# Routed experts of a hybrid decoder step: token rows held in the array while weights stream, 16 weight slots, and sample-token products spread over the array

## The chip, the cores and the metric

The kernel runs on one core of a Trainium2 chip. The metric is the time of one execution on the device in microseconds (us); lower is better. All arithmetic is float32.

## The reference, cut to what matters

Two layers run for a prompt of 256 positions and for 8 sample tokens that carry states and caches: 264 token rows of 1024 values. Layer 0 has a mixer of state-space (SSD) and retention heads, layer 1 a mixer of pooling and convolution. Both then have cross attention to a memory of 256 rows; layer 0 ends in a dense SwiGLU, layer 1 in eight routed experts.

```python
def cross_attn(h, mk, mv, wq, wo):            # sample tokens: mk, mv from a cache per token
    q = (h @ wq).reshape(bsz, seq, X_HEADS, X_HEAD_DIM)
    p = softmax(einsum('blhd,bmhd->bhlm', q, mk) * X_HEAD_DIM ** -0.5)
    return einsum('bhlm,bmhd->blhd', p, mv).reshape(bsz, seq, 1024) @ wo

def moe(h, rw, rb, w1, w3, w2):               # w1, w3: 8 x 1024 x 1792, w2: 8 x 1792 x 1024
    top_v, top_i = lax.top_k(t @ rw + rb, 2)
    gates = softmax(top_v)
    for e in range(8):
        out += combine[:, e:e+1] * ((silu(t @ w1[e]) * (t @ w3[e])) @ w2[e])
```

In layer 0 every sample token b also updates its SSD state (128 x 1024) and its retention state and reads one row of output from each.

## The kernel before, in words

The five engines run programs written by hand, tied by semaphores. PE runs the matrix products; ACT and DVE take results out of PSUM; SP issues nearly all weight loads, POOL those of states, caches and outputs. A float32 product appears in the trace as two matmul records and two weight loads, so counts there are twice those in the code.

**PSUM.** Banks 0 to 5 rotate over named groups in the order of `psum_groups` (`begin`, `end`, `taken`, `full`). Banks 6 and 7 (`SUMS`) hold sums over the sample tokens.

**Weights of the trunk.** `weight_items` lists blocks of 256 columns (1 MB each); SP streams them through six slots of the ring (`TRUNK_RING`), each load waiting until the slot's last block has been used. Slots 6 to 10 hold states and, in cross attention, cache rows (`kv`, five buffers; POOL issues each load at L721 when a buffer is free).

**Sample tokens.** `sample_x` (L968) spreads a token's row over 128 partitions by a product with a column of the identity, in two halves; POOL has decayed the token's state (L676), DVE adds the update, and `sample_y` (L950) multiplies the state by the token's vector, 8 columns wide. `sample_v` and `sample_o` (L1070, L1057) do the same for retention. In `cross`, for every token the query row is spread the same way (L1189) and DVE multiplies it into the cached keys (L2015). In layer 0 the eight parts of the product `xv0` (L1147) are placed between the tokens. After the softmax the probabilities multiply the cached values (L1230): 16 records of 8 x 256 per token. `clear_sums` (L1047) zeroes the sums first, ACT copies them out (`sums_out`, L1473), and the output projection `xo` (L831) follows.

**Experts.** The router's rows are scattered by expert into `expert_rows` in DRAM, 96 rows (`CAP`) for each expert. PE, ACT and DVE loop over four pairs of experts, SP over single experts. For expert n, PE holds a 128 x 64 piece of the weights and streams the 96 token columns of `hg` (L1369), with two such pieces side by side in the array; gate and up come out with hidden units on partitions. ACT takes SiLU (L1606), DVE multiplies (L2210) into `ehid`. PE then turns the next expert's rows (`turn_rows`, L1333), and the down step holds `ehid` and streams the weights: 64 tokens at a time, two column strips side by side (L1387), then the other 32 tokens, four strips side by side (L1393), first for four chunks and then for the other four (`DOWN`). ACT and DVE copy the result out, ACT stores it.

**Chunks.** An expert's weights are 22 chunks (`CHUNKS`): 12 of four k-tiles by 512 columns for gate and up, two of eight k-tiles by 256 columns, eight for down. They pass through 11 slots. SP waits for a slot's release (`expert_left`) and issues the load that reuses it (`expert_load`, L556); the first 11 chunks are loaded while layer 1's attention ends.

Of the kernel before, what the change touches and what calls it, by code (L numbers as in the profile page):

```python
# [29 lines left out]
BLOCKS = ((0, 4), (4, 4), (8, 4), (12, 2))  # L30
DOWN = ((0, 2), (2, 2), (4, 2), (6, 1), (7, 2), (9, 2), (11, 2), (13, 1))
CHUNKS = 22
# [127 lines left out]
def psum_groups():  # L160
# [54 lines left out]
    def cross(l):  # L215
        r = lin_ss(f"xq{l}", KT, CROSS_NORM[l])
        r += [("qs", l, 0), ("qs", l, 1)]
        r += [("S", l, lt, hp) for lt in range(2) for hp in range(2)]
        for b in range(NB):
            r += [("qb", l, b, j) for j in range(2)]  # L220
            if l == 0:
                r += [("xv0", b // 2, b % 2)]
# [20 lines left out]
def trunk_kernel(nc, w, consts, outs):  # L243
# [8 lines left out]
    with ctx:  # L252
# [23 lines left out]
        slot_full = [sem(f"slot_full{s}") for s in range(RING)]  # L276
# [4 lines left out]
        base_full = [16 * sum(i % TRUNK_RING == s for i in range(len(items))) if s < TRUNK_RING else 0 for s in range(RING)]  # L281
# [106 lines left out]
        R.at = max(xr_at, (FT + 2) * T)  # L388
        memtok = R.take(2, DM)
# [38 lines left out]
        R = Region()  # L428
        ehid = R.take(ET, CAP)
        esil = R.take(2, 4, CAP)  # L430
        hg = R.take(2, KT, CAP)
        htok = R.take(3, DM)
        xtok = R.take(3, DM)
        xe = R.take(DM)
        ys = R.take(2, DM)
        back = R.take(2, 3, DM)
        fgain = R.take(DM)
        fin, fsq = view(0, 3, DM), htok[:, 0, :]
# [13 lines left out]
        fss = R.take(3, 1)  # L452
        idx = sb("idx", [P, 3, NE], U32)
# [6 lines left out]
        zeros = small[:, 64:64 + 2 * NB]  # L460
# [44 lines left out]


        @block.sync
        def _(sp):
# [36 lines left out]
            def expert_load(e, j):  # L545

                pick = slice(e, e + 1) if isinstance(e, int) else bass.ds(e, 1)
                if j < 12:
                    b, kh = j // 4, j % 2
                    src, k, n = ups[j % 4 // 2][:, pick, 4 * kh:4 * kh + 4, b * 512:(b + 1) * 512], 4, 512  # L550
                elif j < 14:
                    src, k, n = ups[j - 12][:, pick, :, 1536:1792], 8, 256
                else:
                    f0, k = DOWN[j - 14]
                    src, n = down[:, pick, f0:f0 + k, :], DM
                sp.dma_start(slot_view(j, k, n), src.rearrange("p e t n -> p (e t) n")).then_inc(slot_full[j % RING], 16)  # L556

            def expert_left(n, j):

                if j < 12 and j % 2 == 0:  # L560
                    sp.wait_ge(chunk_done, n * 13 + (j // 2 + 1))
                elif j < 14:
                    sp.wait_ge(sem("up_full" if j in (3, 7, 11, 13) else "gate_full"), n * 4 + (min(j // 4, 3) + 1))
                elif j < CHUNKS - 1:
                    sp.wait_ge(chunk_done, n * 13 + (j - 14 + 7))
                else:
                    sp.wait_ge(sem("down_full"), n + 1)
# [5 lines left out]

            sp.wait_ge(sem("aos_done"), 2)
            for j in range(TRUNK_RING, RING):
                expert_load(0, j)
            for j in range(TRUNK_RING):
                slot_left(sp, last_in_slot[j])
                expert_load(0, j)
# [3 lines left out]
            steps = sp.value_load(rounds[0:1, 1:2], min_val=NE - 1, max_val=3 * NE - 1)  # L583
            with sp.Fori(0, steps) as n:
                e, e_next = n & (NE - 1), (n + 1) & (NE - 1)

                sp.wait_ge(slot_full[0], e + e_next + 1)
                sp.wait_ge(sem("rows_turned"), n + 1)
                rows_load(n + 1)
                for j in range(RING, CHUNKS):  # L590
                    if j != 14:
                        expert_left(n, j - RING + (j == 13))
                    expert_load(e, j)
                for j in range(RING):
                    expert_left(n, j + RING)
                    expert_load(e_next, j)
            sp.wait_ge(sem("rows_turned"), sp.snap(steps + 1))
            rows_load(0)
            for j in range(RING, CHUNKS):
                expert_left(steps, j - RING)  # L600
                expert_load(NE - 1, j)
# [9 lines left out]
        def _(pool):  # L611
# [10 lines left out]
            nc.gpsimd.memset(zeros, 0.0).then_inc(sem("zeros_set"), 1)  # L622
# [129 lines left out]
            load(pw[:, :, :], w["pool_w"][0].rearrange("g c d -> c g d"), "pw_in")  # L752
# [21 lines left out]
            load(fgain, w["norm_final"].unsqueeze(0).to_broadcast([P, DM]), "fgain_in")  # L774
# [9 lines left out]
            for c in range(3):  # L784
                n = P if c < 2 else NB
                for j in range(2):
                    pool.indirect_dma_start(back[0:n, j, c, :], None, xg[:, :], bass.IndirectOffsetOnAxis(ap=rowi[0:n, c, j:j + 1], axis=0))\
# [5 lines left out]
        def _(pe):  # L793
# [101 lines left out]
            pe.wait_ge(sem("dt_ready"), 1)  # L895
# [48 lines left out]
            def sample_y(b):  # L944
# [4 lines left out]
                for g in range(SG):  # L949
                    ins = mm(psum[0:NB, SUMS + g, :], Zc[:, g, b * NB:(b + 1) * NB], hb[:, b % 3, g * 512:(g + 1) * 512],  # L950
                             start=(b == 0), stop=(b == NB - 1), skip_group_check=True)
# [9 lines left out]
            def sample_x(b):  # L961

                if b == 0:
                    taken(pe, ("xstok", 0))
                    taken(pe, ("xstok", 1))
                for g in range(SG):
                    o = begin(("xb", b, g))
                    end(("xb", b, g), mm(o, ident[0:NB, b:b + 1].to_broadcast([NB, P]), xstok[0:NB, g * 512:(g + 1) * 512],  # L968
                                         start=True, stop=True))
# [75 lines left out]
            def clear_sums(n, bank_no):  # L1045

                mm(psum[0:n, SUMS + bank_no, :], zeros[:, 0:n], cbase[:, 0:512], start=True, stop=False, skip_group_check=True)  # L1047

            def sample_o(b):

                taken(pe, ("vb", b))
                if b == 0:
                    pe.wait_ge(sem("q_spread"), 1)
                    pe.wait_ge(sem("zeros_set"), 1)
                    clear_sums(2 * NB, 0)
                for hh in range(RH // 2):
                    ins = mm(psum[0:2 * NB, SUMS, hh * RV:(hh + 1) * RV], Zq[:, hh, b * 2 * NB:(b + 1) * 2 * NB],  # L1057
                             rb[:, b % 4, hh * RV:(hh + 1) * RV], start=False, stop=(b == NB - 1), skip_group_check=True)
# [106 lines left out]
            def cross(l):  # L1165
# [18 lines left out]
                taken(pe, ("qs", l, 0))  # L1184
                taken(pe, ("qs", l, 1))
                for b in range(NB):
                    for j in range(2):
                        o = begin(("qb", l, b, j))
                        end(("qb", l, b, j), mm(o, ident[0:NB, b:b + 1].to_broadcast([NB, P]), qstok[0:NB, j * 512:(j + 1) * 512],  # L1189
                                                start=True, stop=True))  # L1190
                    if l == 0:
                        tokmajor("xv0", [b])
# [30 lines left out]
                clear_sums(NB, 0)  # L1223
                clear_sums(NB, 1)
                taken(pe, ("pT", l))
                for b in range(NB):
                    rows = kv_in(pe, l, NB + b)
                    for h in range(XH):
                        for m in range(2):
                            ins = mm(psum[0:NB, SUMS + h // 2, (h % 2) * 256:(h % 2 + 1) * 256], Zp[:, m * XH + h, b * NB:(b + 1) * NB],  # L1230
                                     rows[:, m, h * 256:(h + 1) * 256], start=False, stop=(b == NB - 1 and m == 1),
# [1044 lines left out]
```

## Time and profile before

| | |
|---|---|
| three timed runs | 1691.6 us median (1689.88 to 1698.04) |
| the profiled execution | 1685.52 us, its span 1683.7 us |
| PE busy | 1540.6 us, 92% of the span |
| HBM read | 339 MB |
| mean granted TensorE clock | 0.947 of full speed |

The profile shows one execution. A chain of waits follows the work that ended last backwards from the end; each piece in it is time that nothing else covered. "Issue" is waiting for which the profile has no event on that engine, such as a DMA's arrival or the fetch of instructions. A window gives the busy time of each engine in a stretch, the granted clock, the DMA engines' busy share (modelled, it can exceed 1) and GB/s.

### The profile page before, as it was taken

The numbers are of one execution on the slowest core, as the hardware profiler recorded it, in microseconds if no ns is written. First come the engines' busy times: TensorE is split into PE (matmuls) and PEld (weight loads), VectorE is DVE, ScalarE is ACT, GpSimd is POOL, SyncE is SP. The second block draws the span as 40 slices with busy tenths as digits, with TensorE's granted clock in tenths as the row PEclk, the third lists the DMA queues.
The fourth block names the chain that finished last, engine by engine and source line by source line (L and its number), as shares of the span: only waits on it lengthen the run. The fifth ranks groups of instructions, "written<-read, shape, count | busy, mean of one in ns | idle before, by whom it ended". The sixth has DMA issues, their size and how long they took to land.

```text
span 1683.7 us, 30260 instructions
## 1 busy us (share of the span) xinstructions
PE 1540.6 (92%) x13352; PEld 1199.3 (71%) x13352; DVE 469.0 (28%) x1264; ACT 183.3 (11%) x382; POOL 125.5 (7%) x156
## 2 busy tenths in 40 slices
PE   7999989899999999999998999959988998998983
PEld 5886557588765888878877764749658667776771
DVE  3436473530340211141278353230000000000002
ACT  2121012101110100000012210020000000000001
POOL 3003412400010200000000001010000000000001
PEclk9997989799999999999999988969999999999997
DMA  9643543554472795435434336638999999999882
GB/s 279 195 152 88 150 113 107 163 188 169 137 269 100 269 393 181 140 107 167 150 128 150 103 110 237 225 124 303 320 362 360 330 351 359 336 344 369 326 320 87
DMA packets 217321, 368.81 MB, mean 219 GB/s; under 512 B 8883, under 2 KB 134091, under 8 KB 217040
## 3 DMA queue, kind: packets, MB, share of 16 engines
q1 hardware_dynamic: 195112, 292.47, 50.5%
q0 software_dynamic: 19264, 71.22, 12.3%
q10 hardware_dynamic: 2816, 3.15, 0.6%
q8 instruction: 112, 1.84, 0.4%
q14 instruction: 17, 0.14, 0.0%
HBM read 339.12 MB, written 28.49 MB: 218 GB/s over the span
## 4 chain that ended last, share of the span: by engine, by line
PE 88%; DVE 5%; issue 4%; POOL 1%; DMA 1%; ACT 1%; ACTq 0%; POOLq 0%; SPq 0%; DVEq 0%
PE psum L831 29%; PE psum L1369 19%; PE psum L1253 9%; PE psum L1147 7%; PE psum L1387 6%; PE psum L1230 3%; PE psum L1393 3%; DVE ring L2015 1%; PE psum L950 1%; PE psum L968 1%; PE psum L1189 1%; PE psum L1215 1%; PE psum L1181 1%; PE psum L986 1%; PE psum L940 1%
## 5 line engine op out<-in xcount | busy, mean ns | idle before, releaser
L1369 PE MATMUL psum<-arena,ring 128*64 128x96 f32 x7168 | 318.6, 252 | 47.1 <-issue 46.2
L1369 PEld LDWEIGHTS psum<-arena,ring 128*64 128x64 f32 x7168 | 310.7, 141 | 56.9 <-issue 56.8
L831 PE MATMUL psum<-hT,ring 128*128 128x264 f32 x1168 | 270.3, 394 | 2.8 <-issue 1.6
L831 PEld LDWEIGHTS psum<-hT,ring 128*128 128x128 f32 x1168 | 224.6, 193 | 48.3 <-issue 7.5
L831 PE MATMUL psum<-arena,ring 128*128 128x264 f32 x992 | 227.0, 392 | 9.3 <-ACT arena L1569 5.0
L831 PEld LDWEIGHTS psum<-arena,ring 128*128 128x128 f32 x992 | 191.3, 193 | 43.8 <-ACT arena L1569 5.8
L1253 PE MATMUL psum<-hT,ring 128*128 128x264 f32 x704 | 157.0, 386 | 0.0
L1253 PEld LDWEIGHTS psum<-hT,ring 128*128 128x128 f32 x704 | 133.8, 190 | 22.9
L1147 PE MATMUL psum<-ring,arena 128*128 128x256 f32 x512 | 113.7, 382 | 0.0
L2210 DVE TENSOR_TENSOR arena<-arena,psum 128x384 f32<-128x384 f32 (+1 forms) x32 | 16.1, 504 | 348.7 <-PE psum L1369 348.7
L1147 PEld LDWEIGHTS psum<-ring,arena 128*128 128x128 f32 x512 | 97.0, 191 | 19.0 <-issue 6.1
L1679 DVE TENSOR_TENSOR arena<-psum,rstd 128x264 f32<-128x264 f32 (+3 forms) x117 | 44.0, 394 | 233.6 <-PE psum L1253 118.8
L1387 PE MATMUL psum<-ring,arena 128*64 128x512 f32 x448 | 99.7, 596 | 0.0
L1387 PEld LDWEIGHTS psum<-ring,arena 128*64 128x64 f32 x448 | 30.7, 137 | 59.0 <-issue 58.1
L1230 PE MATMUL psum<-ring,arena 128*8 128x256 f32 x256 | 55.6, 379 | 0.0
L1685 DVE TENSOR_TENSOR xT<-xT,psum 128x264 f32<-128x264 f32 x40 | 17.2, 429 | 136.1 <-PE psum L831 136.0
L1393 PE MATMUL psum<-ring,arena 128*32 128x256 f32 x896 | 51.7, 381 | 0.0
L2015 DVE CUSTOM_DVE_ANT_0 ring<-ring,psum 128x256 f32<-128x256 f32 x128 | 44.6, 417 | 16.8 <-PE psum L1189 16.8
L1393 PEld LDWEIGHTS psum<-ring,arena 128*32 128x32 f32 x896 | 27.5, 110 | 29.5 <-issue 13.0
L1606 ACT ACTIVATE arena<-psum 128x384 f32<-128x384 f32 (+1 forms) x32 | 14.4, 450 | 305.3 <-PE psum L1369 305.3
L2122 DVE SCALAR_TENSOR_TENSOR arena<-arena,par 128x256 f32<-128x256 f32 x120 | 47.6, 479 | 0.0
L1230 PEld LDWEIGHTS psum<-ring,arena 128*8 128x8 f32 x256 | 23.0, 90 | 33.1 <-issue 1.4
(390 smaller groups left out, 1047.7 us busy)
## 6 DMA issues: line engine op xcount, KB each, us to landing
ring<-in_moe_w_dram SPq DMA_DIRECT2D x160, 1024.0 KB, 9.2
ring<-in_ffn_w_dram SPq DMA_DIRECT2D x30, 1024.0 KB, 5.4
ring<-in_w_in_even_dram SPq DMA_DIRECT2D x22, 1024.0 KB, 5.3
ring<-in_cache_mem_k_dram POOLq DMA_DIRECT2D x16, 1024.0 KB, 8.3
ring<-in_cache_mem_v_dram POOLq DMA_DIRECT2D x16, 1024.0 KB, 5.5
expert_rows<-arena POOLq DMA_DIRECT2D x1, 9216.0 KB, 47.9
ring<-in_w_out_even_dram SPq DMA_DIRECT2D x8, 1024.0 KB, 5.0
ring<-in_xattn_k_dram SPq DMA_DIRECT2D x8, 1024.0 KB, 4.9
```

The costliest lines, as they stand in the source:

```text
L831: ins = mm(outs_[m][0:mw, 0:T], wv[:, k, m * mw:(m + 1) * mw], rhs(base + k), start=(base + k == 0), stop=(kc == len(chunks) - 1 and k == ...
L940: ins = mm(o[:, q * P:(q + 1) * P], ident[0:SH, h:h + 1].to_broadcast([SH, P]), acT[0:SH, c * P:(c + 1) * P], start=True, stop=True)
L1147: ins = mm(o[:, 0:256], mT[:, k, m * P:(m + 1) * P], wv[:, k, :], start=(k == 0), stop=(k == KT - 1))
L1230: ins = mm(psum[0:NB, SUMS + h // 2, (h % 2) * 256:(h % 2 + 1) * 256], Zp[:, m * XH + h, b * NB:(b + 1) * NB], rows[:, m, h * 256:(h + 1) ...
L1253: ins = mm(o[:, 0:T], wv[:, k, m * P:(m + 1) * P], hT[:, k, :], start=(k == 0), stop=(k == KT - 1))
L1369: ins = mm(o[c0:c0 + 64, m * CAP:(m + 1) * CAP], wv[:, k, m * P + c0:m * P + c0 + 64], hg[:, h, kh * kn + k, :], start=(kh == 0 and m == 0 ...
L1387: mm(psum[64 * d:64 * d + 64, 4, :], ehid[:, f0 + f, 0:64], wv[:, f, d * 512:(d + 1) * 512], start=(f0 + f == 0), stop=(f0 + f == ET - 1))
L1393: ins = mm(psum[32 * d:32 * d + 32, 5, 0:256], ehid[:, f0 + f, 64:CAP], wv[:, f, d * 256:(d + 1) * 256], start=(f0 + f == 0), stop=(f0 + f ...
L1679: return v.tensor_tensor(dst, src, rstd[0:src.shape[0], a:b], ALU.mult)
L1685: free((name, t), v.tensor_tensor(xT[:, t, :], xT[:, t, :], bank((name, t))[:, 0:T], ALU.add), wait=True)
L2015: ins = v.tensor_tensor_reduce(kh, kh, bank(key)[:, q * 256:(q + 1) * 256], 1.0, 0.0, ALU.mult, ALU.add, sS[:, m, b * XH + h:b * XH + h + 1])
L2122: v.scalar_tensor_tensor(out=mixo[:, OT + t, 0:NP], in0=gp[:, t, k:k + NP], scalar=gain("ccw", 4 * k + t), in1=mixo[:, OT + t, 0:NP], op0= ...
```

## The change

Gate and up now hold the token rows and stream the weights, as the down step did: first 64 tokens with two strips side by side, then 32 tokens with four. The result has tokens on partitions, so after SiLU and the product PE transposes it (`turn_block`) into the form that the down step needs. Gate and up go in two blocks of 1024 and 768 columns; their chunks are two k-tiles of 1024 or 768 columns, so an expert has 24 chunks. The slots become 16: five more lie in the arena, where earlier buffers are dead; five chunks are loaded before the last attention ends. SP loops over pairs too. Every chunk of gate and up is read twice and released after its second reading.

The sample products are regrouped: where a product has 8 or 16 output rows, its four column quarters go to four strips of 32 output partitions; spread rows are copied by ACT to partitions 32, 64 and 96, and each spreading product takes another strip of input rows. `clear_sums` goes. In layer 0 the parts of `xv0` come after every second token. The gain row of the last norm is loaded under the semaphore on which the router's product waits. Semaphores are merged.

```diff
-BLOCKS = ((0, 4), (4, 4), (8, 4), (12, 2))
-CHUNKS = 22
+BLOCKS = ((0, 1024), (1024, 768))
+DOWN = ((0, 2), (2, 2), (4, 2), (6, 2), (8, 2), (10, 2), (12, 1), (13, 1))
+CHUNKS = 24
+MOE_RING = 16
...
+        slot_at = (mem_at, mem_at + SLOT, tail_at, tail_at + SLOT, 0)
...
+        def picked_row(r, b):
+            return const("ident")[32 * r:32 * r + NB, 32 * r + b:32 * r + b + 1].to_broadcast([NB, P])
...
+                if j < 16:
+                    (f0, n), q = BLOCKS[j // 8], j % 4
+                    src, k = ups[j % 8 // 4][:, pick, 2 * q:2 * q + 2, f0:f0 + n], 2
...
+            full(sp, ("xv1", 3, 1))
+            for j in range(2):
+                expert_load(0, j, j)
+            full(sp, ("wout1", KT - 1))
+            sp.wait_ge(sem("odd_out"), 64)
+            for j in range(2, 4):
+                expert_load(0, j, j)
+            full(sp, ("S", 1, 1, 1))
+            expert_load(0, 4, 4)
             sp.wait_ge(sem("aos_done"), 2)
...
-            load(fgain, w["norm_final"].unsqueeze(0).to_broadcast([P, DM]), "fgain_in")
+            load(fgain, w["norm_final"].unsqueeze(0).to_broadcast([P, DM]), "router_in")
...
-                for g in range(SG):
-                    ins = mm(psum[0:NB, SUMS + g, :], Zc[:, g, b * NB:(b + 1) * NB], hb[:, b % 3, g * 512:(g + 1) * 512],
+                for j in range(4):
+                    ins = mm(psum[32 * j:32 * j + NB, SUMS, 0:256], Zc[:, j // 2, b * NB:(b + 1) * NB],
...
+                    r = 2 * (b % 2) + g
+                    end(("xb", b, g), mm(o, picked_row(r, b), xstok[32 * r:32 * r + NB, g * 512:(g + 1) * 512], start=True, stop=True))
...
-                    if l == 0:
-                        tokmajor("xv0", [b])
+                    if l == 0 and b % 2:
+                        tokmajor("xv0", [b - 1, b])
...
-                clear_sums(NB, 0)
-                clear_sums(NB, 1)
...
-                    for h in range(XH):
-                        for m in range(2):
-                            ins = mm(psum[0:NB, SUMS + h // 2, (h % 2) * 256:(h % 2 + 1) * 256], Zp[:, m * XH + h, b * NB:(b + 1) * NB],
+                    for m in range(2):
+                        for h in range(XH):
+                            ins = mm(psum[32 * h:32 * h + NB, SUMS, 0:256], Zp[:, m * XH + h, b * NB:(b + 1) * NB],
...
-            pe.wait_ge(sem("router_in"), 32)
+            pe.wait_ge(sem("router_in"), 48)
...
+                    def up_block(g, b):
+                        f0, fn = BLOCKS[b]
+                        j0 = 8 * b + 4 * g
+                        wide, narrow = fn // 2, fn // 4
+                        for q in range(4):
+                            arrive(j0 + q)
+                            wv = weights(j0 + q, 2, fn)
+                            for k in range(2):
+                                for c in range(2):
+                                    mm(psum[64 * c:64 * c + 64, 3 * b + g, 0:wide], hg[:, h, 2 * q + k, 0:64],
+                                       wv[:, k, c * wide:(c + 1) * wide], start=(q == 0 and k == 0), stop=(q == 3 and k == 1))
+                        for q in range(4):
+                            wv = weights(j0 + q, 2, fn)
+                            for k in range(2):
+                                for c in range(4):
+                                    ins = mm(psum[32 * c:32 * c + 32, 3 * b + 2, g * 256:g * 256 + narrow], hg[:, h, 2 * q + k, 64:CAP],
+                                             wv[:, k, c * narrow:(c + 1) * narrow], start=(q == 0 and k == 0),
+                                             stop=(q == 3 and k == 1), skip_group_check=True)
+                            if q < 3:
+                                ins.then_inc(chunk_done, 1)
...
+                    up_block(0, 0)
+                    up_block(1, 0)
+                    up_block(0, 1)
+                    turn_block(0)
+                    up_block(1, 1)
+                    pe.wait_ge(sem("ys_low"), n + 1)
+                    pe.wait_ge(sem("ys_high"), n + 1)
+                    down_part(0)
+                    turn_block(1)
                     pe.wait_ge(sem("rows_in"), n * 16 + 32)
                     turn_rows()
+                    down_part(1)
...
-                src = psum[0:n, SUMS:SUMS + banks, :].rearrange("p a b -> p (a b)")
-                af(dst[0:n, :], src, ACT.Copy).then_inc(sem("sums_out"), 1)
+                for j in range(4):
+                    ins = af(dst[0:n, j * width:(j + 1) * width], psum[32 * j:32 * j + n, SUMS, 0:width], ACT.Copy)
+                ins.then_inc(sem("sums_out"), 1)
...
+                taken(act, ("qs", l, 0))
+                taken(act, ("qs", l, 1))
+                for r in range(1, 4):
+                    af(qstok[32 * r:32 * r + NB, :], qstok[0:NB, :], ACT.Copy).then_inc(sem("q_copied"), 1)
```

`turn_block` transposes four or three 128 x 128 pieces of the 64-token rows and two or four of the 32-token rows; ACT then copies the first into `ehid`, DVE the second.

## Rows read from the trace of the kernel before

**Rows 1.** The page: busy time, and the chain's share by line.

```profile
PE 1540.6 (92%) x13352; PEld 1199.3 (71%) x13352; DVE 469.0 (28%) x1264; ACT 183.3 (11%) x382; POOL 125.5 (7%) x156
...
PE psum L831 29%; PE psum L1369 19%; PE psum L1253 9%; PE psum L1147 7%; PE psum L1387 6%; PE psum L1230 3%; PE psum L1393 3%; DVE ring L2015 1%; PE psum L950 1%; PE psum L968 1%; PE psum L1189 1%; PE psum L1215 1%; PE psum L1181 1%; PE psum L986 1%; PE psum L940 1%
```

**Rows 2.** Groups by line and shape: busy us, mean ns of one | idle before.

```profile
L1369 PE MATMUL psum<-arena,ring 128*64 128x96 f32 x7168 | 318.6, 252 | 47.1 <-issue 46.2 <-DVE arena L2198 0.9
...
L1387 PE MATMUL psum<-ring,arena 128*64 128x512 f32 x448 | 99.7, 596 | 0.0
...
L1393 PE MATMUL psum<-ring,arena 128*32 128x256 f32 x896 | 51.7, 381 | 0.0
...
L2015 DVE CUSTOM_DVE_ANT_0 ring<-ring,psum 128x256 f32<-128x256 f32 x128 | 44.6, 417 | 16.8 <-PE psum L1189 16.8
...
L1057 PE MATMUL psum<-ring 128*16 128x128 f32 x64 | 11.7, 346 | 5.7 <-DVE ring L1901 5.6
```

**Rows 3.** Windows of the expert stage: engines' busy us, clock, DMA share, GB/s.

```profile
1136.60:1656.70 520.10, 473.89 (x8576) 374.51 (x8576) 23.58 (x47) 27.19 (x51) 0.00 (x0) 0.97 0.92 330
...
1224.00:1236.00 12.00, 10.46 (x248) 10.11 (x246) 0.56 (x1) 0.49 (x1) 0.00 (x0) 1.00 1.03 408
...
1211.00:1215.00 4.00, 2.58 (x63) 2.39 (x57) 0.00 (x0) 0.49 (x1) 0.00 (x0) 1.00 1.03 247
1249.00:1251.00 2.00, 2.00 (x44) 1.23 (x40) 0.00 (x0) 0.00 (x0) 0.00 (x0) 1.00 0.06 7
```

**Rows 4.** Chain in the expert stage: start us, us, what.

```profile
1223.01 5.50 PE psum L1369 x127
...
1241.86 0.81 PE psum L1333 x8
1242.67 6.16 PE psum L1387 x28
1248.83 3.16 PE psum L1393 x56
...
1261.30 5.46 issue
```

**Rows 5.** Chain through the values product of layer 1.

```profile
1033.28 1.81 PE psum L1047 x4
1035.10 27.64 PE psum L1230 x128
...
1062.76 1.02 ACT arena L1473
```

**Rows 6.** Timeline: the first cache load that waits for that product.

```profile
1038.86 0.70 POOL L721 DMA_DIRECT2D ring<-in_cache_mem_v_dram  x1 [14.16 <-PE psum L1230]
```

**Rows 7.** The tile ring, 980 to 1066 us: its loads' landing.

```profile
DMA to landing us min/median/max: 5.2/5.4/13.7
```

**Rows 8.** Chain in layer 0's attention: scores, then the query spread and xv0.

```profile
440.78 6.91 PE psum L1181 x32
447.69 1.91 PE psum L1189 x4
449.60 3.65 PE psum L1147 x16
```

**Rows 9.** Chain in the SSD stage: spread rows and state products.

```profile
163.91 3.14 PE psum L950 x4
...
199.06 1.91 PE psum L968 x4
200.97 1.81 PE psum L950 x4
```

**Rows 10.** Timeline: the gain row's load.

```profile
1097.78 0.58 POOL L613 DMA_DIRECT2D arena<-in_norm_final_dram  x1
```

**Rows 11.** Line 613 from 1090 to 1130 us: landing of its three loads.

```profile
DMA to landing us min/median/max: 6.1/6.4/7.5
```

**Rows 12.** Chain: the router's product.

```profile
1103.46 3.56 PE psum L1301 x16
```

More of the change, by code:

```diff
@@ L280, in trunk_kernel @@
         xg_slots = xg.rearrange("(n s) d -> s n d", s=CAP)
-        base_full = [16 * sum(i % TRUNK_RING == s for i in range(len(items))) if s < TRUNK_RING else 0 for s in range(RING)]
+        base_full = [16, 48, 16 * 13] + [0] * (MOE_RING - TRUNK_RING - 3)
+        base_full += [16 * sum(i % TRUNK_RING == s for i in range(len(items))) for s in range(TRUNK_RING)]
         class Region:
@@ new lines, in turn_block @@
+                    def turn_block(b):
+                        pe.wait_ge(sem("hid_tok"), n * 2 + (b + 1))
+                        for t in range(BLOCKS[b][1] // 256):
+                            tr(psum[:, 3 * b, t * P:(t + 1) * P], tok64[b][:, t * P:(t + 1) * P], ident)
+                        if b == 0:
+                            for t in range(2):
+                                ins = tr(psum[:, 1, t * P:(t + 1) * P], tok32[0][:, t * P:(t + 1) * P], ident)
+                        else:
+                            at = TOK32_B
+                            tr(psum[:, 4, 0:P], arena[:, at:at + P], ident)
+                            tr(psum[:, 4, P:2 * P], arena[:, at + 64:at + 192], ident)
+                            tr(psum[0:64, 4, 2 * P:3 * P], arena[:, at + 128:at + 192], ident)
+                            ins = tr(psum[:, 4, 3 * P:4 * P], arena[:, at - 64:at + 64], ident)
+                        ins.then_inc(sem("hid_turned"), 1)
@@ new lines, in down_part @@
+                    def down_part(part):
+                        j0 = 16 + 4 * part
+                        pe.wait_ge(sem("ehid_64"), n * 2 + (part + 1))
+                        pe.wait_ge(sem("ehid_32"), n * 2 + (part + 1))
+                        for q, (f0, fn) in enumerate(DOWN[4 * part:4 * part + 4]):
+                            arrive(j0 + q)
+                            wv = weights(j0 + q, fn, DM)
+                            for f in range(fn):
+                                for d in range(2):
+                                    mm(psum[64 * d:64 * d + 64, 6, :], ehid[:, f0 + f, 0:64], wv[:, f, d * 512:(d + 1) * 512],
+                                       start=(f0 + f == 0), stop=(f0 + f == ET - 1))
+                        for q, (f0, fn) in enumerate(DOWN[4 * part:4 * part + 4]):
+                            wv = weights(j0 + q, fn, DM)
+                            for f in range(fn):
+                                for d in range(4):
+                                    ins = mm(psum[32 * d:32 * d + 32, 7, 0:256], ehid[:, f0 + f, 64:CAP], wv[:, f, d * 256:(d + 1) * 256],
+                                             start=(f0 + f == 0), stop=(f0 + f == ET - 1))
+                            ins.then_inc(sem("down_full") if part and q == 3 else chunk_done, 1)
```

287 lines of the change are left out of this document (135 added, 152 removed).

## The prediction

> **What bounds the kernel now.** I read the page first: PE is busy for 92% of the span, and the chain that ends last lies on PE's lines almost throughout [rows 1]. So PE time that nothing else covers is worth its full price; what matters is where PE works and where it only waits. Then the groups by line: they show that almost all of PE's idle time in the expert stage stands in front of L1369, 46.2 of 47.1 us as "issue", that is, waits for a DMA or for instructions [rows 2]. Third, the windows of that stage: it takes 520.1 us, at 330 GB/s on average [rows 3]. In a stretch in which, by SP's order, down chunks pass (rows of 4 KB), the DMA engines move 408 GB/s; in one in which the two chunks of 256 columns (rows of 1 KB) pass, 247 GB/s at about the same busy share; and at 1249 us, early in a down part, they move 7 GB/s while PE works: all 11 slots are held, and none is released before the part's second reading [rows 3]. Last the chain, for the length of each piece at full clock [rows 4, 5, 8, 9].
>
> So the expert stage is bound by PE and DMA in turn. PE's own work for an expert: 896 records of L1369 at 5.50/127 = 43.3 ns, 38.8 us; down 2 x (6.16 + 3.16) = 18.6; `turn_rows` 0.8 [rows 4]. Together 58.2, times eight 466. The other 54 us of the 520 are 47 idle and some 8 at the half clock, 1.2 GHz (mean granted clock 0.97 [rows 3]; L1369 is busy for 318.6 us [rows 2], at 43.3 ns it would be 310.4). Of the 47, three stops of some 5.4 us stand where PE's loop goes back [rows 4], 16.3 in all; 30 are waits for weights.
>
> **Part 1, gate and up the other way round.** The new product is that of the down step, so its price is that of L1387 and L1393. Block 0, gate: 8 k-tiles x 2 strips x 2 records = 32 of 512 columns at 6.16/28 = 0.220, 7.04 us; 64 of 256 columns at 3.16/56 = 0.0564, 3.61 us [rows 4]. Gate and up: 21.3. Block 1 has three quarters of the columns: 16.0 if the time goes with the columns, 21.3 if not at all. A pair of records of L1369 takes 86.7 ns for 96 columns, 0.90 ns a column; one of L1387 440 ns for 512, 0.86. So it goes with the columns nearly down to 96: I take 16.1. Thirteen transposes at 0.81/8 = 0.10, a little more for 128 columns than for 96: 1.5. Down 18.6 and `turn_rows` 0.8 stay. Sum 58.3 against 58.2: **the product itself gives nothing**; it was already packed.
>
> New waits. `turn_block(0)` waits for SiLU and product of block 0, while PE has the whole gate of block 1 (8 us) before it; `turn_block(1)` has the first down part (10.7) before it. Behind `turn_block(1)` only `turn_rows` (0.8 us) covers one ACT copy and four short DVE copies. Queued behind this wait is the second down part, and behind that the next expert. I take 1.0 us an expert for this and for starting transposes; the bounds are 0 and 3 (every copy exposed at about 0.5).
>
> On changes of shape the rows say this: in a down part PE goes from two strips to four and back, and still pays 0.86 to 0.88 ns a column, less than L1369, which does not change shape [rows 4]. The Trainium skill, TensorEngine Tiling (Array Packing), Key Properties, says that changing the tiling mode drains the engine, and the new order has some 16 such changes in an expert where there were about six. It gives no price there; by the rows it is too small to see, and the sum keeps none.
>
> **Part 2, chunks and slots.** An expert is 22.02 MB; at 408 GB/s [rows 3] 54.0 us, below PE's 59.3. The rows of 1 KB go; 768 columns make rows of 3 KB, which the trace does not have. Bounds: 408 and 247 GB/s for these 6.29 MB, so 54.0 to 64.0 us; I take the upper rate, since the stretch with 408 has rows of 4 KB and only rows of 1 KB were slow. Sixteen slots hold 14.7 MB when the stage begins, so 161.5 MB are left: 396 us at 408 GB/s, and 466 with the slow price for 3 KB. PE needs 475. The phase at work holds four slots; twelve may run ahead of it, against seven before, so a dead time as at 1249 us should not come back. The 30 us of waits go.
>
> The loop still goes back three times: 16.3 stay. The half clock's 8.2 I also keep. SP now goes back three times instead of seven; its queue holds over ten chunks, some 30 us of DMA, so a stop of SP is covered. Early loads (five chunks behind the trunk's last weights, in SP's order) go out while layer 1's scores are made; they cost nothing unless they delay cache rows, by 2.6 us for one of 1 MB.
>
> Stage: 8 x 59.3 + 16.3 + 8.2 = 499 against 520: **-21** (-30 to +5).
>
> **Part 3, values product (L1230), both layers.** Now 1.81 + 27.64 us lie on the chain alone [rows 5]. In four strips a token's 16 records cost 16 x 0.0564 = 0.90, as four strips do in L1393, 7.2 for eight. But there are five buffers: the loads for tokens 5, 6 and 7 go out only when tokens 0, 1 and 2 are done. What is late next is that DMA: the first issue came 0.3 us after token 0 was done (1035.10 + 27.64/8 = 1038.56, issued at 1038.86 [rows 5, 6]); then 5.4 to landing [rows 7]. So 0.9 + 0.3 + 5.4 = 6.6, two more at 2.6 each (1.05 MB at 408), 11.8, last token 12.7. Four ACT copies instead of one of 1.02 [rows 5]: +0.5 (0 to 3). PE idles between the last tokens, so I charge 2 us of half clock for the start of the projection. 29.4 - 12.7 - 0.5 - 2 = 14.2 a layer: **-28** (-18 with a landing of 13.7 [rows 7] in both layers, -32 at best).
>
> **Part 4, spread of the query in layer 0.** PE alternates 1.91 and 3.65 [rows 8]. Four products now use four strips of input rows. No row shows that such strips overlap; column strips do. Bounds for two tokens: 3.82 as now, 0.96 if all four overlap; times four, 0 to -11.5. With overlap in twos it is -7.6; I take **-9**, since column strips come close to full overlap. DVE's 8 x 0.35 us a token [rows 2], 5.6 for two, stays below PE's 8.3. In layer 1 DVE is the bound: nothing. The three ACT copies (3.1 us at 1.02 [rows 5]) hide behind the scores, 6.91 [rows 8]; without that cover they would cost 3.1 a layer. The Trainium skill, TensorE: Matmul & The Clock Gate, Part 3, reports a speedup of 3.07 for four row tiles of 512 columns; by that the estimate is 3.82 - 1.24, times four, -10.3. No run here shows it yet.
>
> **Part 5, SSD and retention.** `sample_y` 1.81 becomes 8 x 0.0564 = 0.45, `sample_x` 1.91 becomes 0.96 if two overlap [rows 9]. In two steps the product takes 3.14 because PE waits for DVE there; what lies before that wait gives nothing, nor does token 0. Six of eight y and five of eight x count: 8.2 + 4.8, less 1.4 for token 7, whose product must wait for DVE's update: **-11** (-5 to -13). Retention: L1057 is busy for 11.7 us, three quarters could go, but half of its tokens wait for DVE and POOL: **-3.5** (0 to -8).
>
> **Part 6, the gain row.** The router's product now waits for it: issued at 1097.78, landing at most 7.5 later [rows 10, 11], 1105.3, against a start at 1103.46 [rows 12]: **+1.8** (0 to +2). The rest (merged semaphores, the fill that goes) is off PE's path.
>
> **Sum.** -21 - 28 - 9 - 11 - 3.5 + 1.8 = -70.7. The profiled execution took 1685.5 us, 1.8 more than its span; after: 1615. The runs' median lies 6.1 higher, 1691.6; on it the forecast is **1621 us**.
>
> **Rivals.**
> *Strips of input rows do not overlap.* For: nothing in the trace shows that they do. Parts 4 and 5 lose 9 + 4.8: 1635.
> *The expert stage gains nothing*, since the short cover behind `turn_block(1)`, or 3 KB rows at 247 GB/s, take the 30 us again. For: 466 us of DMA would leave little room beside PE's 475. Against: four slots of 16 held, 408 GB/s. 1621 + 21 = 1642.
> *Slower: the new rows load badly.* The place is the stage's DMA. The other parts save 50, so it decides from 570 us for 161.5 MB, 284 GB/s. At 247 for all rows: 654 us, 134 more than now: 1691.6 + 134 - 50 = 1776. Against: 408 GB/s with rows of 4 KB.
> *The loop's going back is cheaper too*, since PE's loop is shorter and the DMA engines less full: up to -16, 1605.
>
> **How the numbers follow.** Chances: forecast 0.60, strips 0.15, stage without gain 0.15, slower 0.03, cheaper loop 0.07. The range from 1602 to 1648 takes in all of these but the slow one; some tail is left out on either side, where two of them fall together or a part reaches its bound. Half a per cent, 8 us, is about what a measurement of this kernel can tell from no change. Faster 0.95, same 0.02, slower 0.03.
>
> **What would show it.** In the new profile: the stage at about 499 us with idle time before gate and up only where the loop goes back; no window near 7 or 247 GB/s; the values product at 12 to 14 us with gaps before tokens 5 to 7; four spread products in about 1 to 1.9 us; the router's product about 2 us later after the norm. Wrong it would be if the new gate and up pay more than 0.9 ns a column, if PE still waits for chunks, or if products on other strips of input rows follow one another.

## The result, and the profile after

The changed kernel takes 1621.7 us (median of four runs, 1619.0 to 1627.2); the kernel before, beside it, 1692.2 (1689.9 to 1698.0). The ratio is 0.9589, with a 95% interval from 0.957 to 0.961. The forecast was 1621, but the hit is partly luck: several of its steps were wrong or mis-sized, and their errors nearly cancel.

The profiled executions tell a little less than the medians: 1685.5 before and 1627.2 after, 58.3 us apart, where the medians are 70.5 apart. The profiled execution after was the slowest of its four. A second profile of the same kernel (the run "again" below) has a span of 1613.9 instead of 1625.4, and like the profile before it lies some 6 us below its median.

The page after (busy time; the chain's share by engine; PE's instruction packets: number, MB, share):

```profile
PE 1481.6 (91%) x9382; PEld 1020.6 (63%) x9382; DVE 477.1 (29%) x1304; ACT 201.2 (12%) x419; POOL 125.5 (8%) x155
...
q8 instruction: 80, 1.31, 0.3%
...
PE 86%; DVE 6%; issue 2%; DMA 2%; POOL 1%; ACT 1%; ACTq 0%; POOLq 0%; SPq 0%; DVEq 0%
```

The chain is still PE's [rows 1], with 9,382 instructions of PE instead of 13,352. Matching events of the traces give where the 58.3 us came from, beside the terms of the sum; the last column is the second profile:

| part | forecast | measured | second profile |
|---|---|---|---|
| expert stage, 520.1 to 491.5 (488.3) | -21 | -28.6 | -31.8 |
| values product, two layers (-11.7, -10.1; then -11.6, -14.9) | -28 | -21.8 | -26.5 |
| query spread, layer 0 | -9 | -11.2 | -11.2 |
| SSD and retention | -14.5 | +1.7 | +0.2 |
| gain row | +1.8 | +0.3 | +0.1 |
| elsewhere | 0 | +1.3 | -0.8 |
| sum | -70.7 | -58.3 | -69.8 |

So one kernel's parts differ by up to 5 us from one execution to the next, and a smaller difference in one part tells nothing.

**Expert stage.** The window of the stage after, with the columns of [rows 3]:

```profile
1106.17:1597.68 491.51, 475.94 (x4584) 213.68 (x4584) 31.17 (x87) 34.26 (x67) 0.00 (x0) 0.98 0.90 342
```

PE is busy for 475.9 us, 2 more than before [rows 3]: the product itself gives nothing, as forecast. What went is idle time. The waits of the stage after, in total, times, longest:

```profile
PE psum L1390 <- issue: 14.0, 3, 5.1
```

The three are where PE's loop goes back; the chain shows one, and the half clock behind it (10.09 us for 32 records that take 7.02 elsewhere):

```profile
1225.48 5.05 issue
1230.53 10.09 PE psum L1390 x32
```

**Values product**, chain of layer 0: the first token, the wait for the last token's load, the last token, the transposes of the sums, then the projection. [rows 5] has the same place in layer 1 before.

```profile
493.95 1.09 PE psum L1252 x16
...
497.18 8.41 DMA ring<-in_cache_mem_v_dram
...
505.64 1.94 PE psum L1252 x16
...
509.28 1.01 PE psum L990 x8
...
510.59 31.61 PE psum L863 x128
```

**Query spread**, chain of layer 0, the four products of two tokens; the xv0 products between take 7.10 for two. [rows 8] has 1.91 for the two of one token:

```profile
466.34 1.07 PE psum L1214 x8
```

**SSD.** The second of its four steps, before and after, as the chain has it: spread rows (L968, L1000), state products (L950, L982), decay rows (L940, L972), y products (L986, L1017), the state's product (L997, L1028), the z projection. Before:

```profile
156.50 1.91 PE psum L968 x4
158.41 1.81 PE psum L950 x4
160.22 1.98 PE psum L940 x16
...
167.06 2.24 PE psum L986 x16
169.30 0.91 PE psum L997 x2
170.21 7.12 PE psum L831 x32
177.33 1.91 PE psum L968 x4
```

After:

```profile
156.92 1.06 PE psum L1000 x4
157.98 0.55 PE psum L982 x8
158.53 1.10 PE psum L972 x8
...
164.23 3.65 PE psum L1017 x16
167.87 1.81 PE psum L1028 x2
169.68 8.16 PE psum L863 x32
177.85 1.06 PE psum L1000 x4
```

The regrouped products are as short as forecast, and the y products start 7.3 us after the step's beginning instead of 10.6. But the step takes 20.9 us, as before (20.8): from the y products on everything is longer. The windows of that step after, from the decay rows on (granted clock third from the end), say why:

```profile
159.63:164.23 4.60, 2.64 (x21) 1.06 (x20) 4.55 (x13) 1.47 (x3) 3.80 (x3) 0.70 1.07 314
164.23:169.68 5.45, 5.45 (x19) 4.42 (x20) 3.07 (x5) 0.00 (x0) 2.87 (x3) 0.50 0.33 80
169.68:177.85 8.17, 8.17 (x35) 6.50 (x33) 0.69 (x1) 0.39 (x1) 1.39 (x1) 0.88 0.38 114
```

In the first window VectorE is busy for 4.55 of 4.60 us and PE for 2.64: PE waits for the decay products. Then the clock is at 0.50, 1.2 GHz, while PE works without a gap.

### The profile page after: what moved, and what is told of

Same layout as the page of the kernel before. It is cut to its first block, busy times and chain, and to the rows that moved or that the text cites. A ratio compares the mean times of both kernels' runs of the same rounds, so it can differ in the third digit from the quotient of the medians.

```text
span 1625.4 us, 22293 instructions
## 1 busy us (share of the span) xinstructions
PE 1481.6 (91%) x9382; PEld 1020.6 (63%) x9382; DVE 477.1 (29%) x1304; ACT 201.2 (12%) x419; POOL 125.5 (8%) x155
## 4 chain that ended last, share of the span: by engine, by line
PE 86%; DVE 6%; issue 2%; DMA 2%; POOL 1%; ACT 1%; ACTq 0%; POOLq 0%; SPq 0%; DVEq 0%
PE psum L863 31%; PE psum L1390 13%; PE psum L1275 10%; PE psum L1172 7%; PE psum L1396 6%; PE psum L1429 6%; PE psum L1435 3%; DVE ring L2083 1%; DMA ring<-in_cache_mem_v_dram 1%; PE psum L1239 1%; PE psum L1206 1%; PE psum L1017 1%; DVE ring L1873 1%; PE psum L1407 1%; PE psum L1323 0%
## 5 line engine op out<-in xcount | busy, mean ns | idle before, releaser
L1390 PE MATMUL psum<-ring,arena 128*64 128x384 f32 (+1 forms) x704 | 137.2, 541 | 0.0
L1390 PEld LDWEIGHTS psum<-ring,arena 128*64 128x64 f32 x704 | 49.1, 137 | 80.0 <-issue 80.0
L1390 PE MATMUL psum<-arena 128*64 128x512 f32 (+1 forms) x320 | 72.1, 602 | 14.8 <-issue 14.0
L2277 DVE TENSOR_TENSOR arena<-arena,psum 128x512 f32<-128x512 f32 (+1 forms) x16 | 9.9, 621 | 252.1 <-PE psum L1396 252.1
L1396 PE MATMUL psum<-ring,arena 128*32 128x256 f32 (+1 forms) x1408 | 71.4, 354 | 0.0
L1429 PE MATMUL psum<-ring,arena 128*64 128x512 f32 x288 | 64.4, 594 | 0.8 <-issue 0.8
L1396 PEld LDWEIGHTS psum<-ring,arena 128*32 128x32 f32 x1408 | 44.1, 110 | 30.2 <-issue 11.3
L1390 PEld LDWEIGHTS psum<-arena 128*64 128x64 f32 x320 | 23.7, 149 | 56.5 <-issue 56.5
L1429 PEld LDWEIGHTS psum<-ring,arena 128*64 128x64 f32 x288 | 22.2, 137 | 37.1 <-issue 35.7
L819 POOL DMA_INDIRECT arena<-expert_rows,rowi x6 | 5.6, 934 | 505.9 <-ACTq L1691 504.4
```

Of the source, the lines that this page charges most:

```text
L1390: mm(psum[64 * c:64 * c + 64, 3 * b + g, 0:wide], hg[:, h, 2 * q + k, 0:64], wv[:, k, c * wide:(c + 1) * wide], start=(q == 0 and k == 0), ...
L1396: ins = mm(psum[32 * c:32 * c + 32, 3 * b + 2, g * 256:g * 256 + narrow], hg[:, h, 2 * q + k, 64:CAP], wv[:, k, c * narrow:(c + 1) * narro ...
L1429: mm(psum[64 * d:64 * d + 64, 6, :], ehid[:, f0 + f, 0:64], wv[:, f, d * 512:(d + 1) * 512], start=(f0 + f == 0), stop=(f0 + f == ET - 1))
```

## The experiments

Each is compared with the kernel before in runs beside it; 1689.6 to 1690.9 us is its median there. Edits are shortened. The order follows the questions.

**The SSD stage: theory A, the half clock takes the gain; rival B, something else costs it.** Three kernels, the first the changed one once more.

> The changed kernel once more, unaltered, as the measure for the three kernels that run beside it on the same chip. Both theories expect 1617 to 1625 us, the SSD stage ending (start of the first g projection) at about 227 us of the span.

Measured: 1622.0 us, ratio 0.9601 (0.9581 to 0.9622).

> The sample products of the SSD stage alone are put back as they were before (both spread rows and both state products on one strip, one wide copy of the sums, no copies of the sample rows); all else as changed. Theory A, that PE now waits for VectorE in this stage and pays the time saved back at the half clock: within 3 us of the changed kernel, SSD stage ending at 225 to 228 us, spread rows 1.9 and state products 1.8 us again, y products 1.9 to 2.3 and z products 7.1 again. Rival B, that the regrouping saves its 11 us and something else that was changed beside it costs as much: 11 us slower than the changed kernel, stage ending at 238.

```diff
-for j in range(4):
-    mm(psum[32*j:32*j+NB, SUMS, 0:256], Zc[:, j//2, ...], hb[:, b%3, j*256:(j+1)*256], ...)
+for g in range(SG):
+    mm(psum[0:NB, SUMS+g, :], Zc[:, g, ...], hb[:, b%3, g*512:(g+1)*512], ...)
-pe.wait_ge(sem("x_copied"), 3)
-mm(o, picked_row(r, b), xstok[32*r:32*r+NB, ...], ...)
+mm(o, picked_row(0, b), xstok[0:NB, ...], ...)
```

Measured: 1621.2 us, ratio 0.9594 (0.9572 to 0.9616): no difference from the changed kernel, where B asked for 11 us. B falls by the time. In its profiled execution the stage ends later than A had it, at 231 us (226.9 and 225.5 in the two profiles of the changed kernel), with y products of 3.61 in the second step: the clock can drop there with the old products too.

> The changed kernel, and on PE ahead of each wait for VectorE's decay products 9, 9, 4 and 3 idle products of 128 x 256 into an unused bank (some 0.4 us each at full clock), whose results nothing reads. Theory A (the half clock after the wait takes the gain): y products 3.65 to about 2.0, z products of the first two steps 8.2 to 7.1, stage ending 7 to 10 us earlier than in the changed kernel, at 217 to 220 us; what of that reaches the end is 5 to 10 us, unless the retention stage waits for GpSimd's stores anyway (then less). Rival B (it is not the clock): the fillers only add work, 0 to 3 us slower.

```diff
+fill((9, 9, 4, 3)[s])   # mm(psum[:, SUMS+1, 0:256], ident, cbase[:, 0:256], start=True, stop=True)
 for j in range(2):
     pe.wait_ge(sem("s_ready"), 2 * s + j + 1)
```

Measured: 1614.9 us, ratio 0.9562 (0.9542 to 0.9582), 7.2 us faster than the changed kernel. The windows of the same step:

```profile
161.29:165.38 4.09, 4.09 (x21) 3.63 (x21) 4.05 (x7) 0.83 (x2) 1.54 (x1) 1.00 0.75 218
165.38:168.02 2.64, 2.64 (x19) 2.16 (x19) 1.30 (x2) 0.00 (x0) 0.49 (x1) 1.00 0.02 8
168.02:175.14 7.12, 7.12 (x34) 5.80 (x33) 0.69 (x1) 0.39 (x1) 3.77 (x3) 1.00 0.52 147
```

PE even starts the y products 1.8 us later (9.1 us behind the step's beginning), but at full clock they and the state's product take 2.64 us instead of 5.45, the projection 7.12 instead of 8.17, the step 18.8 instead of 20.9. The stage ends at 220.5 us. A holds: useless work in a wait buys the time that the regrouping had earned.

> As the kernel with fillers in the SSD stage, and 4, 3, 3 fillers ahead of the cache waits of tokens 5, 6 and 7 of the values product in both layers and 4 ahead of the transposes of its sums. Theory A: the output projection after it takes 28.8 us instead of 31.6 and 31.3, the last token's products and the transposes go at full clock: 3 to 4 us a layer, 6 to 8 us faster than with the SSD fillers alone. Rival: the loads end the product and the projection is slow for another reason, such as its weights: no difference.

```diff
+fill((0, 0, 0, 0, 0, 4, 3, 3)[b])
 rows = kv_in(pe, l, NB + b)
 ...
+fill(4)
 o = begin(("aoT", l))
```

Measured: 1611.1 us, ratio 0.9541 (0.952 to 0.9562), the fastest version; 3.8 us faster than the SSD fillers alone, against 6 to 8 expected. The projection runs at full clock in both layers; layer 0:

```profile
504.94 28.75 PE psum L863 x128
```

What lies ahead of it is not shorter in layer 0: from the end of the prompt's attention product to the projection 17.8 us instead of 17.3, although the last token takes 1.05 us instead of 1.94. So the loads set it.

**The values product.**

> The values product of both layers alone is put back: its 128 products on one strip with 8 output rows each into two banks, one wide copy of the sums. Theory, from the changed kernel's trace (V product gave 11.7 and 10.1 us): 20 to 24 us slower than the changed kernel, product 27.6 us on the chain, output projection at full clock, 28.8 us. By the prediction's term: 28 slower. Rival, that the loads of tokens 5 to 7 would have bound the product of before as well: no difference.

```diff
-for m in range(2):
-    for h in range(XH):
-        mm(psum[32*h:32*h+NB, SUMS, 0:256], ...)
+for h in range(XH):
+    for m in range(2):
+        mm(psum[0:NB, SUMS + h//2, (h%2)*256:(h%2+1)*256], ...)
```

The two clearing products ahead of it are left out, so that half of the sample tokens' sums lack a part. Measured: 1642.1 us, ratio 0.9713 (0.9684 to 0.9741), 20 us slower than the changed kernel; 27.81 us for the product and 28.75 for the projection of layer 0. The clearing products, 1.81 us a layer [rows 5], belong to the term of 28 and are absent here; with them the term is worth some 24, not 28.

**The query spread.**

> The spread of the query alone uses one strip of input rows (rows 0 to 7) for all four products of two tokens; xv0 still comes after every second token. If strips of input rows overlap, as the changed kernel's trace reads (four products in 1.07 us): the four take 3.8 us, 11 us slower. If the gain of the phase came from asking xv0 for two tokens at a time: no difference.

Measured: 1637.5 us, ratio 0.9676 (0.9644 to 0.9707), 15.5 us slower. Chain of layer 0:

```profile
463.51 3.62 PE psum L1214 x8
...
477.86 8.79 PE psum L1172 x32
```

Four products on one strip of input rows take 3.62, on four strips 1.07: strips of input rows overlap almost fully. What lies beyond the 11 stands in the xv0 products, 8.8 to 9.5 us in three of four places instead of 7.1, at a granted clock of 0.75 to 0.81 (1.00 in the changed kernel) although PE has no gap there. The Trainium skill, TensorE: Matmul & The Clock Gate, Part 3, reports a speedup of 3.07 for four row tiles; the traces give a little more, 3.62/1.07 = 3.4.

**The expert stage: slots, rows, or the product's order?**

> The expert stage as changed, except that SP issues a chunk only when the chunk eleven places ahead of it has been released, as with 11 slots, instead of sixteen (the first 16 chunks are loaded as changed). If the stage's gain of 28 us comes from the number of slots: waits for weights return, 15 to 30 us slower, stage 505 to 520 us. If it comes from longer rows or the product's order: within 5 us, stage 491.

```diff
 def expert_left(p, i):
+    i += 5
```

Measured: 1623.2 us, ratio 0.960 (0.9572 to 0.9628); stage 491.7 us. Eleven slots do as well as sixteen.

> The changed kernel, with the gate and up chunks loaded in rows of 1 KB and 768 bytes instead of 4 and 3 KB, by two DMAs a chunk (40 issues an expert instead of 24); the products are the same. If rows of 1 KB go at the 247 GB/s of the window before, as the prediction took as its slow bound: 77 us of DMA an expert against 59 of PE, stage 560 to 580 us, 70 to 90 us slower. If that window was slow only because little was asked for there: within 10 us of the changed kernel.

Measured: 1626.0 us, ratio 0.9602 (0.9569 to 0.9635); stage 493.7. A window in which the queue of the weights carries only rows of 1 KB and 768 bytes:

```profile
1150.00:1170.00 20.00, 19.80 (x183) 9.06 (x183) 1.69 (x6) 1.47 (x3) 0.00 (x0) 1.00 1.10 353
```

353 GB/s, where the prediction took 247 [rows 3] as the price of such rows. They cost this stage nothing that can be told from one execution to the next. The 247 was a misreading of the trace before, as its packets by size show, first for 1211 to 1215 us, then for 1217 to 1220:

```profile
DMA packets 461, 0.99 MB, mean 247 GB/s; under 512 B 16, under 2 KB 20, under 8 KB 460
DMA packets 1037, 1.05 MB, mean 349 GB/s; under 512 B 16, under 2 KB 1036, under 8 KB 1037
```

The slow window carried rows of 2 KB and more; why it was slow is open. The rows of 1 KB came behind it, at 349 GB/s.

> The expert stage with the new chunks, rows and sixteen slots, but gate and up multiplied as before (weights held, 96 token columns streamed, 896 products of 64 output rows an expert, no transposes after). If the product itself gives nothing, as the prediction has it: stage within 6 us of the changed kernel's 491. If the gain comes from the product's new order: stage 510 to 520, 20 to 28 us slower.

```diff
-for c in range(2):
-    mm(psum[64*c:64*c+64, 3*b+g, 0:wide], hg[:, h, 2*q+k, 0:64], wv[:, k, c*wide:(c+1)*wide], ...)
+for m in range(fn // P): for k in range(2): for c0 in (0, 64):
+    mm(psum[c0:c0+64, first + m//4, m%4*CAP:...], wv[:, k, m*P+c0:m*P+c0+64], hg[:, h, 2*q+k, :], ...)
```

Measured: 1633.5 us, ratio 0.9649 (0.9616 to 0.9682); stage 503.8, 12.3 more than after, between the two expectations. PE is busy for 470.4, less than after; it waits more:

```profile
PE psum L1391 <- issue: 33.4, 22, 4.5
```

So the old product's order brings stops back (21 us beside the 12.4 of the loop's going back), with the weights' sixteen slots in place. The trace of before, read again, has this chain:

```profile
1340.28 5.50 PE psum L1369 x127
1345.78 1.94 issue
1347.71 12.43 PE psum L1369 x254
1360.14 0.30 issue
1360.44 5.50 PE psum L1369 x128
1365.94 1.02 issue
```

The stops stand every 127 or 128 records (a chunk is 64), in one expert behind 63, 190, 317 and 444 records, drifting against the chunks. And the weights were there: worked out from the trace's landings for 101 chunks of gate and up, each had landed 13.6 to 25.8 us before its first product. One that a stop stands in front of, at 1234.53, was issued at 1203.8; the view of the tile ring for that issue says when it landed:

```profile
DMA to landing us min/median/max: 16.9/16.9/16.9
```

1220.7, 14 us before the stop. What does arrive then is PE's instructions. The page of before:

```profile
q8 instruction: 112, 1.84, 0.4%
```

112 packets of 16 KB against 80 after; before, one starts at 1213.45, 1220.51, 1226.66 and 1232.82 us, and stops end at 1216.34, 1223.01, 1229.04 and 1235.54, 2.4 to 2.9 us behind. All 36 stops over 0.2 us in this stage end so, 2.3 to 3.1 us behind the start of a packet, and the three where the loop goes back are among them; in the kernel with the old product all 22 do, 2.4 to 2.8 us behind. Not every packet brings a stop: the first expert has one, the second six, and while L1369 runs packets start 4.1 to 8.3 us apart. The Trainium skill, Advanced Engine Details and Errata, ISA Cache, gives a line as 16 KB, 256 instructions; 127 products with their weight loads are 254, so the trace agrees. By that figure, an estimate, 112 packets hold 28,672 instructions, where PE has 26,704 records, and 80 hold 20,480, where it has 18,764 after: these are PE's packets. Theory C follows.

> The changed kernel, but each wide gate and up product of the expert stage is cut into products of 64 columns (block 0) and 96 columns (block 1); the same weights, chunks, waits and sums, and 1,226 PE records an expert instead of 570. Theory C, that the stops of the stage before were PE's own instructions arriving (one 16 KB packet for each 127 records, some 6.1 us apart at best, against 5.5 us of work at 43 ns a record): stops come back in front of every 127th record inside these products, some 0.5 to 1 us in block 1 and more in block 0, though every chunk has landed; stage 40 to 110 us longer. Theory D, that the stops of before were waits for weights, which sixteen slots end: no stops but the loop's three; the stage longer only by what short products cost PE itself (at 43 ns a record no more than some 10 us an expert in block 0, none in block 1).

```diff
-mm(psum[64*c:64*c+64, 3*b+g, 0:wide], ..., wv[:, k, c*wide:(c+1)*wide], ...)
+for i in range(0, wide, 64 if b == 0 else 96):
+    mm(psum[64*c:64*c+64, 3*b+g, i:i+step], ..., wv[:, k, c*wide+i:c*wide+i+step], ...)
```

Measured: 1678.9 us, ratio 0.9938 (0.9912 to 0.9965); stage 547.5, 56 longer than after. Waits, and the chain behind one turn of the loop:

```profile
PE psum L1392 <- issue: 46.7, 22, 4.5
```

```profile
1236.93 2.50 PE psum L1392 x41
1239.42 3.02 issue
1242.45 8.25 PE psum L1392 x215
...
1254.28 6.92 PE psum L1392 x232
1261.20 1.90 issue
```

Stops are back, in each turn of the loop behind the same records: 488 of this line in the first expert of a pair and, from the second turn on, 41; 228 and 420 in the second expert. Each ends 2.2 to 2.5 us behind the start of a packet. A chunk of block 0 has 64 records here, so all four places are in the middle of chunks, where PE waits for no weight. In block 1 there is a single stop, against what C had expected of 43 ns a record. Stops beyond the 14.0 after are 33 of the 56 us; the other 23 are the price of short products (8.25 us for 215 of them). D falls; C holds as to the cause, not as to each place, nor with its packets 6.1 us apart at best.

> The kernel with sixteen slots and the gate and up product of before, its four gate chunks of block 1 loaded in rows of 1 KB by two DMAs each. If short rows ahead of them hold up PE's instruction packets: the stops of PE become longer where these chunks pass, 2 to 3 us as in the second half of each pair before, 5 to 20 us slower than that kernel (stage above 508). If the stops do not depend on what the DMA engines carry: stage 504 as in that kernel.

Measured: 1633.3 us, ratio 0.965 (0.9615 to 0.9685); stage 501.5. The stops do not grow with short rows beside them.

**Further fillers.**

> The kernel with fillers in the SSD stage and the values product, and further: GpSimd holds its load, store and product of one sample state until VectorE's decay products of the third SSD step are done; fillers in PE's waits before the last two rotations of layer 0 and before the last spread products and the attention product of layer 1. If VectorE's 4.1 us product is so long because GpSimd works beside it (0.65 us otherwise): that product takes 0.65 us and the step ends 2 to 4 us earlier. With the half clock avoided at the first g projection after the rotations and at layer 1's attention product (9.6 and 9.8 us to 7.3 and 7.1): 5 us. Together 4 to 9 us faster than the kernel with both kinds of fillers; a rival is that retention waits for GpSimd anyway and only layer 1's 2.7 us are left.

```diff
+if b == 4: pool.wait_ge(sem("s_ready"), 6)    # GpSimd, ahead of hload(b + 2)
+if i == 6: fill(11)                           # rotations
+if l and b > 5: fill(5)                       # spread, layer 1
+if l: fill(4)                                 # twice, ahead of layer 1's attention product
```

Measured: 1623.4 us, ratio 0.9593 (0.9566 to 0.9619): 12 us slower than the kernel that it builds on. The hold was put at the wrong token, and VectorE's long product still meets GpSimd's work, so that this question was not tried. The projection behind the rotations still takes 9.6 us. Layer 1's attention product did take 6.9 us instead of 9.8, but the fillers ahead of it, at the half clock, cost as much: from the start of the scores to its end 45.7 us instead of 45.9. The loss is elsewhere: the expert stage, whose code is the same, takes 504.4 us instead of 488.4. Chain of the kernel that it builds on, then its own:

```profile
1212.46 4.05 issue
1216.51 8.78 PE psum L1398 x32
```

```profile
1214.69 4.15 issue
1218.84 2.35 PE psum L1408 x5
1221.18 3.16 issue
```

From the second turn on each has a second stop, after five records: 9.4 us in all, and PE's products behind them go slower, at a granted clock of 0.965 over the stage instead of 0.985. These stops too end 2.2 to 2.4 us behind the start of a packet, so they are waits for instructions. That the added instructions moved the loop against the 16 KB packets would explain it; it was not tried by itself.

## Why the prediction was right, and where it was not

**Product, "gives nothing": right for PE's work, not for the stage.** 58.6 us an expert in the trace after against 58.2 and 58.3 worked out, and four strips and two alternate without a visible cost. But its half number of records ends stops, which the prediction put down to the slots.

**"The 30 us of waits go", "30 are waits for weights": the first half right, the second wrong.** This is a failed step: "issue" was read as a DMA although the row names none. The weights had been there for 13 us or more. The stops were waits for PE's own instructions, at a record each 43 ns; the new product has half the records, and only the three stops of the loop remain. That the 54.0 us of DMA an expert, the rows of 3 KB and the slots decide was wrong with it: 11 slots and rows of 1 KB cost nothing, and the 247 GB/s were not those of rows of 1 KB. Of the stage's 28.6 us the product's order gives 12.3, shown by the kernel with the old product. The other 16.3 came with the rest of the rewrite; 13 of them are less waiting for instructions, 46.2 [rows 2] to 33.4. Neither slots nor rows were seen to give them, and the same loop has differed by 16 us with 29 products more ahead of it. What in the rewrite gave them stays open.

**SSD, -11 (its own terms add up to 11.6): wrong, and retention, -3.5, with it.** The step failed that charged each shortened product at its full price. The products did shrink, and PE reached the y products 3.2 us earlier, but what is late next is VectorE; PE now idles there, and at 1.2 GHz the y products (+1.4), the state's product (+0.9) and the projection (+1.0) give back 3.3. In retention, the chain lies on GpSimd and VectorE from the fourth token on, before as after, so that shorter products give nothing there, and one projection takes 10.1 us instead of 7.3. In the fourth step of SSD a VectorE product takes 4.1 us instead of 0.65 while GpSimd issues two DMAs and multiplies (201.84 to 206.11); before, the same GpSimd work began at 203.52, when it was over. In the kernel with the old sample products it began behind it as well, at 209.38, and two such products took 1.28. The Trainium skill, SBUF — State Buffer, Who interferes with whom, says that a VectorE instruction with two SBUF inputs contends with a GpSimd one that reads SBUF, under an exclusive lock. The rows fit that in part: GpSimd's product began at 204.20, 1.65 us behind VectorE's, which was late by then. No run moved GpSimd's work alone: argued, not shown.

**Values product, -28: right in kind, too large.** The copies took 0.5 more, as charged, and the last load landed after 11.6 and 12.4 us, 11.8 charged. Mis-sized is the half clock: the last token takes 1.9 us instead of 0.9, and in layer 0 the transposes and the projection lose 3.3 us, for 2 charged. In layer 1 the projection before had lost 1.7 to it already (30.5), and after it takes 31.3; the prompt's attention product pays as well, 10.0 us instead of 7.1, at a granted clock of 0.71. In the second profile layer 1's last token and projection go at full clock (1.09 and 28.8), and the term comes to 26.5; so part of the miss is one execution's.

**Query spread, -9: right**; strips of input rows overlap more fully than it took them to. **Gain row, +1.8: smaller**, 0.3.

The rival with strips that do not overlap falls by the run on one strip, that of slow rows by the run with 1 KB. The loop's going back is not cheaper by much: 14.0 and 12.7 us in the two profiles instead of 16.2.

## What to carry to other kernels

Time that PE saves in front of another engine's wait can come back as half clock behind it; ask what is late next, and if it is not PE, a few useless products in the wait may be worth more than the saving. "Issue" with no DMA named is worth a count of the records between two stops and a look at the loads' landing: here a constant number that was not the chunk's pointed at instructions, and fewer, longer products helped where buffers did not. Before a window's rate is put down to one kind of row, its packets are worth reading by size.

## What was not expected of the hardware

PE's instructions come in 16 KB packets. Code that uses one in 5.5 us had 33 stops of 0.3 to 2.8 us in the stage before, besides those where the loop goes back, and every one ends 2.3 to 2.9 us behind the start of a packet. The same loop took 488.4 or 504.4 us, with 29 useless products more ahead of it.
